# First part of both feed-forward stages: a buffer for each sum of squares, the roots taken together, the down weights split later, some sums and low parts on GpSimd

## The reference

```python
def rmsnorm(x, g, eps=1e-6):
    y = x * lax.rsqrt(jnp.mean(x * x, axis=-1, keepdims=True) + eps)
    return y * g

def swiglu(h, wg, wu, wd):
    return (jax.nn.silu(h @ wg) * (h @ wu)) @ wd
...
x = x + swiglu(rmsnorm(x, norm_ffn[layer]), w_gate[layer], w_up[layer], w_down[layer])
```

## Time and profile before

| | us |
|---|---|
| median of 3 runs (3134.54 to 3141.05) | 3136.88 |
| the profiled execution | 3135.46 |
| its span, first to last instruction | 3133.7 |

### The profile page before, as it was taken

One profiled execution on the slowest core, in us unless ns is written; L12 is line 12 of the kernel. 1 busy time (PEld: TensorE's weight loads), 2 busy tenths in 40 slices (PEclk: granted clock), 3 DMA queues, 4 the chain that ended last, 5 costly groups with the idle time before them and its releaser, 6 DMA issues. The chain is left out here.

```text
span 3133.7 us, 47003 instructions
## 1 busy us (share of the span) xinstructions
PE 2995.8 (96%) x18884; PEld 2917.1 (93%) x18884; DVE 1277.0 (41%) x2761; ACT 960.0 (31%) x1653; POOL 816.3 (26%) x434
## 2 busy tenths in 40 slices
PE   6999997999899999999989999999999999999998
PEld 5889987899899999999989999999889999999997
DVE  4423345566533333323353444444653333333334
ACT  4322234444521111111154444444452112111112
POOL 3211112111233222222232223322213223323220
PEclk8999998999999999999999999999999999999999
DMA  3122143110212111111021111111112111211101
GB/s 119 58 69 64 49 168 102 51 54 25 74 41 61 46 40 54 40 40 40 13 69 39 46 45 45 43 42 43 34 38 77 41 40 46 61 40 40 54 0 64
DMA packets 199615, 165.75 MB, mean 53 GB/s; under 512 B 9766, under 2 KB 182774, under 8 KB 199294
## 3 DMA queue, kind: packets, MB, share of 16 engines
q1 hardware_dynamic: 199486, 163.96, 17.3%
HBM read 140.78 MB, written 28.92 MB: 54 GB/s over the span
## 5 line engine op out<-in xcount | busy, mean ns | idle before, releaser
L1402 DVE TENSOR_TENSOR xT<-xT,ffn_banks 128x384 f32<-128x384 f32 (+1 forms) x528 | 280.0, 532 | 219.1 <-PE ffn_banks L238 218.6
L236 PE MATMUL ffn_banks<-hhi,ffn_whi 128*128 128x384 f32 (+1 forms) x1056 | 346.6, 328 | 12.4 <-DVE ffn_act L1382 12.4
L236 PE MATMUL ffn_banks<-hhi,whi 128*128 128x384 f32 (+1 forms) x1056 | 347.8, 329 | 4.1 <-DVEq L1367 3.7
L238 PE MATMUL ffn_banks<-hhi,wlo 128*128 128x384 f32 (+1 forms) x1056 | 346.2, 328 | 0.0
L236 PE MATMUL ffn_banks<-ffn_ahi,ffn_whi 128*128 128x384 f32 (+1 forms) x1056 | 344.7, 326 | 1.6 <-DVE xT L1402 1.6
L237 PE MATMUL ffn_banks<-hlo,whi 128*128 128x384 f32 (+1 forms) x1056 | 346.0, 328 | 0.0
L237 PE MATMUL ffn_banks<-hlo,ffn_whi 128*128 128x384 f32 (+1 forms) x1056 | 345.7, 327 | 0.0
L238 PE MATMUL ffn_banks<-hhi,ffn_wlo 128*128 128x384 f32 (+1 forms) x1056 | 345.5, 327 | 0.0
L238 PE MATMUL ffn_banks<-ffn_ahi,ffn_wlo 128*128 128x384 f32 (+1 forms) x1056 | 344.2, 326 | 0.0
L237 PE MATMUL ffn_banks<-ffn_alo,ffn_whi 128*128 128x384 f32 (+1 forms) x1056 | 344.1, 326 | 0.0
L1288 POOL TENSOR_TENSOR ffn_alo<-ffn_act,ffn_ahi 128x384 fp32r<-128x384 f32 (+1 forms) x132 | 127.9, 970 | 776.6 <-ACT ffn_ahi L1209 776.6
(11 more groups left out here) (363 smaller groups left out, 6740.1 us busy)
## 6 DMA issues: line engine op xcount, KB each, us to landing
ffn_up_st<-in_w_up SPq DMA_DIRECT2D x44, 512.0 KB, 3.8
ffn_down_st<-in_w_down SPq DMA_DIRECT2D x22, 1024.0 KB, 4.8
wst<-in_w_gate SPq DMA_DIRECT2D x24, 512.0 KB, 3.7
wst<-in_w_qkv SPq DMA_DIRECT2D x23, 512.0 KB, 4.4
wst<-in_w_in SPq DMA_DIRECT2D x22, 512.0 KB
ffn_gate_st<-in_w_gate SPq DMA_DIRECT2D x20, 512.0 KB
wst<-in_w_out SPq DMA_DIRECT2D x16, 512.0 KB
load_xin<-in_x_prompt SPq DMA_DIRECT2D x8, 512.0 KB, 4.8
```

Of the source, the lines that this page charges most:

```text
L236: nc.tensor.matmul(out, whi[:, k, :], hhi[:, k, c0:c0 + w], start=(k == 0), stop=False)
L238: last = nc.tensor.matmul(out, wlo[:, k, :], hhi[:, k, c0:c0 + w], start=False, stop=(k == kts - 1))
L1402: v.tensor_tensor(x, x, banks[:, 4 + k % 4, 0:w], ALU.add).then_inc(added, 1)
```

## The change

Part 0 of both feed-forward stages is put in another order on four engines.

- Each chunk's sum of squares has a buffer of its own: `acc`, and two that lie in the staging of the up weights (`up_st`). So the squares wait no longer for `total` of the chunk before. Instead ScalarE waits, ahead of the squares of chunk 1, for GpSimd's low parts of both up tiles, and SyncE sends the up weights of part 1 only when all three totals are made.
- ScalarE: squares of chunk 1, root 0, high parts of chunk 2, squares of chunk 2, roots 1 and 2 together; only then Silu and the high parts of the first chunk's hidden values. The split of the down weights stands between the two Silu of the second chunk.
- GpSimd: takes the low part of gate tile 1 (`split(0, 0, 1)`), which VectorE made, and the three sums of chunk 2. The low parts of the first chunk's hidden values stand ahead of the down weights' low part.
- TensorE: `total(1)` stands behind the first group of the second chunk and `total(2)` behind its second group.
- VectorE: the low parts of chunk 1 ahead of reciprocal 0, the sums of chunk 1 ahead of the first scaling, the low parts of chunk 2 and reciprocals 1 and 2 ahead of the first product.

```diff
@@ Rms.square
             if q == 0:
-                dst = self.acc
-                if i:
-                    act.wait_ge(self.summed, i)
+                dst, m = self.acc[i % len(self.acc)], len(self.acc)
+                if i >= m:
+                    act.wait_ge(self.summed, i - m + 1)
@@ Rms.add
-    def add(self, dve, i):
+    def add(self, engine, i, on):
...
-            a = self.acc[:, :, 0:w]
-            self.nc.vector.tensor_tensor(a, a, self.sq[n % 2][:, :, 0:w], ALU.add).then_inc(self.added, 1)
+            a = self.acc[i % len(self.acc)][:, :, 0:w]
+            on.tensor_tensor(a, a, self.sq[n % 2][:, :, 0:w], ALU.add).then_inc(self.added, 1)
@@ ffn_stage
-                  acc, [banks[:, 4], banks[:, 5]], r)
+                  [acc[:], *(up_st[:, f, 0:2 * W].rearrange("p (k n) -> p k n", n=W) for f in range(F))], [banks[:, 4], banks[:, 5]], r)
@@ SyncE, loads
                             sp.wait_ge(w_lo[m], lo_count(m, i - 1, f))
+                        if m and isinstance(i, int):
+                            sp.wait_ge(rms.summed, NC)
                         load(i, m, f)
@@ ScalarE
             for k in range(KT):
                 gained_high(nc, S, g0, k, order[1]).then_inc(x_hi, 1)
+            act.wait_ge(w_lo[1], lo_count(1, 0, F - 1))
+            rms.square(act, 1)
             rms.root(act, 0)
-            rms.square(act, 1)
             for k in range(KT):
                 gained_high(nc, S, g0, k, order[2]).then_inc(x_hi, 1)
+            rms.square(act, 2)
+            rms.root(act, 1)
+            rms.root(act, 2)
+            hidden(0, [0])
+            silu(0, 1, 0)
+            split_down(0)
+            silu(0, 1, 1)
             for f in range(F):
-                silu(0, 0, f)
-            for f in range(F):
-                high(0, 0, f)
-            rms.root(act, 1)
-            rms.square(act, 2)
-            split_down(0)
-            hidden(0, [1])
-            rms.root(act, 2)
+                high(0, 1, f)
             hidden(0, [2])
@@ GpSimd
+            split(0, 0, 1)
             for f in range(F):
                 split(0, 1, f)
+            rms.add(pool, 2, nc.gpsimd)
+            hidden(0, [0])
             split_down(0)
-            hidden(0)
+            hidden(0, [1, 2])
@@ TensorE
             for f in range(F):
                 for m in range(2):
                     group(0, 1, f, m)
-                rms.total(pe, 1 + f)
+                    if f == 0:
+                        rms.total(pe, 1 + m)
@@ VectorE
-            dve.wait_ge(w_hi[0], 1)
-            v.tensor_tensor(wlo[0][:, 1, :], gate_st[1], whi[0][:, 1, :], ALU.subtract).then_inc(w_lo[0], 1)
-            rms.add(dve, 0)
-            rms.reciprocal(dve, 0)
+            rms.add(dve, 0, v)
             for k in range(KT):
                 dve.wait_ge(x_hi, k + 1)
                 gained_low(nc, S, g0, k, order[1]).then_inc(x_lo, 1)
+            rms.reciprocal(dve, 0)
+            rms.add(dve, 1, v)
             dve.wait_ge(rms.rooted, 1)
             for f in range(F):
                 scale_gate(0, 0, f)
                 scale_up(0, 0, f)
-            rms.add(dve, 1)
-            for f in range(F):
-                multiply(0, 0, f)
             for k in range(KT):
                 dve.wait_ge(x_hi, KT + k + 1)
                 gained_low(nc, S, g0, k, order[2]).then_inc(x_lo, 1)
             rms.reciprocal(dve, 1)
-            rms.add(dve, 2)
-            dve.wait_ge(rms.rooted, 2)
+            rms.reciprocal(dve, 2)
+            for f in range(F):
+                multiply(0, 0, f)
+            dve.wait_ge(rms.rooted, 3)
+            dve.wait_ge(product, F)
             hidden(0, [1])
-            rms.reciprocal(dve, 2)
-            dve.wait_ge(rms.rooted, 3)
             hidden(0, [2])
```

More of the change, by code:

```diff
@@ L1043, in add @@
             n = 3 * i + q - 1
-            dve.wait_ge(self.squared, 4 * i + q + 1)
+            engine.wait_ge(self.squared, 4 * i + q + 1)
             if n:
-                dve.wait_ge(self.added, n)
-            a = self.acc[:, :, 0:w]
-            self.nc.vector.tensor_tensor(a, a, self.sq[n % 2][:, :, 0:w], ALU.add).then_inc(self.added, 1)
+                engine.wait_ge(self.added, n)
+            a = self.acc[i % len(self.acc)][:, :, 0:w]
+            on.tensor_tensor(a, a, self.sq[n % 2][:, :, 0:w], ALU.add).then_inc(self.added, 1)
     def total(self, pe, i):
@@ L1055, in total @@
         for k in range(2):
-            last = self.nc.tensor.matmul(self.means[i % n][:, 0:w], self.S["ones"][:], self.acc[:, k, 0:w],
+            last = self.nc.tensor.matmul(self.means[i % n][:, 0:w], self.S["ones"][:], self.acc[i % len(self.acc)][:, k, 0:w],
                                          start=(k == 0), stop=(k == 1))
@@ L1281, in split_down, with hidden @@
                 nc.gpsimd.tensor_tensor(flat[1], down_st[:], flat[0], ALU.subtract).then_inc(w_lo[2], 1)
-            def hidden(i):
-                for c, (c0, w) in enumerate(CH):
+            def hidden(i, cs=range(NC)):
+                for c in cs:
+                    c0, w = CH[c]
                     for f in range(F):
@@ L2428, in mix1_stage @@
         rms = Rms(nc, S, st, (0, 1, 2), [vflat[:, j * 2 * W:(j + 1) * 2 * W].rearrange("p (k n) -> p k n", n=W) for j in range(2)],
-                  otok[:].rearrange("p a n -> p (a n)")[:, 0:2 * W].rearrange("p (k n) -> p k n", n=W), [pP[:, 0], pP[:, 1]], r)
+                  [otok[:].rearrange("p a n -> p (a n)")[:, 0:2 * W].rearrange("p (k n) -> p k n", n=W)], [pP[:, 0], pP[:, 1]], r)
         block = st.block()
@@ L2853, in _ @@
             nc.vector.memset(nb[CHUNK:P, 0:CHUNK], BIG).then_inc(s["set_up"], 1)
-            rms.add(dve, 0)
+            rms.add(dve, 0, nc.vector)
             rms.reciprocal(dve, 0)
-            rms.add(dve, 1)
+            rms.add(dve, 1, nc.vector)
             for n, x in enumerate(ahead):
@@ L2859, in _ @@
                     rms.reciprocal(dve, 1)
-                    rms.add(dve, 2)
+                    rms.add(dve, 2, nc.vector)
                 if n == 4 * KT:
```

## The result

The changed kernel took 3118.3 us (median of 4 runs, 3117.07 to 3118.78) against 3138.1 us for the kernel before, run beside it: a ratio of 0.9939, 95% interval 0.9926 to 0.9952, that is 19 us less (by the ratio; by the medians 19.8). Its profiled span is 3117.0 us, 16.7 us shorter than before.

The account below looks back on a forecast made before the run. TensorE, busy for 96% of the span, was taken as the bound. Gains of 7.5 us in `ffn0` and 11.2 us in `ffn1`, together 18.7 us off 3136.9, gave 3118.2 us, range 3110 to 3126 us.

Parts of the forecast that it names:

- Both old waits go: TensorE's waits for `total(2)` and second-chunk `scale_up` vanish: 4.0 and 4.25 us in `ffn0`, 2.7 and 8.15 us in `ffn1`.
- on offer: TensorE's old waits plus half-clock losses in part 0, all that could be gained: 13.1 us in `ffn0`, 13.65 us in `ffn1`.
- The margin of 1.3 us: After `total(2)`, TensorE has 8.4 us of work to cover the 7.1 us until `scale_gate` of chunk 2 is done.
- GpSimd holds VectorE up: GpSimd's SBUF reads block VectorE at stage start: first sum near 1.8 us, first two low parts near 1.4 and 2.7 us.
- Side by side: Rival: GpSimd and VectorE don't hold each other up at stage start; gain 25.3 us, 3111.6 us; chance 0.20.
- The chain to `scale_gate`: From TENSOR_SCALAR to the first scaling, through root and table load, 6.8 us as in `mix1`, 0.5 shorter in `ffn0`.
- the new waits: TensorE waits for the first `scale_gate` in each stage: 4.25 us in `ffn0`, 2.45 us in `ffn1`.
- Clock: Half clock on TensorE behind the new waits: 1.7 us charged in `ffn0` (3.1 at most), nothing in `ffn1` (2.8 at most).
- GpSimd's sums: Third chunk's three adds on GpSimd, 1.85 us each for 768 columns; no wait at `total(2)` finally charged.
- The slower rival: GpSimd's three adds hold TensorE at `total(2)`; 5.5 us an add eats the gain, 6.6 us makes it 6 us slower; chance 0.04.
- Sum: Net gain in part 0: 7.5 us in `ffn0` and 11.2 us in `ffn1`, together 18.7 us, giving 3118.2 us.

Follow-up runs that it names:

- e8: e7 plus gate tile 1's low part back on VectorE and the third chunk's squares ahead of its high parts; 3116.4 us, 0.9938 of the kernel before.
- e5: The changed kernel with one more, unneeded GpSimd subtraction reading SBUF behind the up low parts; 3122.7 us in one run.
- e6: The changed kernel with an unneeded GpSimd fill with zeros, reading no SBUF tensor, behind the up low parts; 3119.2 us in one run.
- e9: e8 with VectorE's reciprocal 1 ahead of the third chunk's low parts and reciprocal 2 after four of them; 3116.0 us, 0.9914 of the kernel before.
- e7: The changed kernel with root 0 ahead of the second chunk's fourth square and the first scaling behind its first sum; 3118.5 us, 0.9940 of the kernel before.
- e10: The changed kernel measured again, unaltered, beside e9 on the same chip; 3125.3 us, 0.9947 of the kernel before.
- e3: The changed kernel with the third chunk's three sums on VectorE, behind that chunk's low parts; 3121.5 us, 0.9943 of the kernel before.
- e2: The changed kernel with one buffer for the three sums, as before the change; 3130.0 us, 0.9973 of the kernel before.

## Why the prediction was right

- **Both old waits go.** They went, with the half clock behind them: 13.1 and 13.65 us on offer. The margin of 1.3 us behind `total(2)` held in the changed kernel: `scale_gate` of chunk 2 ends 1.0 us before TensorE needs its bank in `ffn0` (838.50 against 839.49) and 1.3 us in `ffn1`. e8 shows how soon it is used up (3.4 us of waiting once the reciprocals came late).
- **GpSimd holds VectorE up.** Shown by the lengths (first sum 1.78 us, predicted 1.8; first two lows 4.15 us, predicted 1.4 + 2.7) and by e5 against e6. "Side by side" fell with it: 25 us were not reached, and e9, which takes the collisions and the chain out of TensorE's way, gets 13 us out of `ffn0` and 13.8 out of `ffn1`, all that was on offer.
- **The chain to `scale_gate`.** 6.7 us where the earlier trace rows gave 6.8; the new waits are 4.17 and 2.21 us, predicted 4.25 and 2.45. e7 shows that square, sum and table load are 2.8 us of it. Of the drain that the Trainium skill adds to a table load ("ScalarE: Activation LUTs", section "What ACT_TABLE_LOAD costs") the trace shows nothing again: load 2318.85 for 1.28, Sqrt at 2320.15.
- **Clock.** 1.7 us charged in `ffn0`, 1.7 us measured; nothing charged in `ffn1`, nothing measured. This was partly luck: in e10 the same kernel lost 1.6 us there as well, and 3.0 us in `ffn0`, close to the 3.1 that the prediction gave as the most.
- **GpSimd's sums.** 1.9 us an add of 768 columns, 1.6 of 640 (busy time by line), near the 1.85 that I took; with ScalarE's last square between them three take 6.0 us, and `total(2)` waited in neither stage. In `ffn0` it missed a wait by 0.3 us (the last sum ends at 829.54, `total(2)` starts at 829.87), and only because the half clock had made TensorE late, as the prediction has it. The slower rival needed 5.5 us an add.
- **Sum.** 7.5 and 11.2 us predicted, 7.9 and 11.4 measured; 3118.2 us predicted, 3118.3 measured. So close a hit has luck in it: medians of one kernel differ by 3 to 7 us from chip to chip here (before 3136.5 to 3143.0, changed 3118.3 and 3125.3). Two slips in the working change nothing: 827.6 against 826.7 is 0.9 us late, not 1.0; and the adds of `ffn1` start at 2331.2 in the slower rival, by which three of them end near 2335.8, not 2336.3.

## What to carry to other kernels

When an elementwise step moves to GpSimd, look at what VectorE does meanwhile: if both read their operands from SBUF, and VectorE's instruction has two of them there, VectorE's waited here until GpSimd's had ended, and the price was that wait, not GpSimd's slower pace. An instruction with one SBUF operand, such as the reciprocal of e9, can be put beside GpSimd's. When a wait on the busiest engine shrinks, look at the next thing in its list at once: here the first scaling, `total(2)` and the third chunk took the same 2 to 4 us over from one another until all three were early. Undo the parts one by one: one moved line alone gave about half of the gain, taking the separate buffers away lost about half, and the sums on GpSimd gave nothing that could be told.

## What the runs showed of the hardware

VectorE's instructions with two SBUF inputs that met a subtraction of GpSimd's ended 0.36 us (320 columns), 0.42 us (384) and 0.8 us (768) after it; a fill by GpSimd held up none, and a reciprocal beside its sums kept its length.

Every feed-forward stage starts with TensorE idle for 1.8 to 1.9 us. In 19 of the 24 starts of these twelve profiles the clock then fell to 1.2 GHz for a while and 1.6 to 1.7 us were lost; in 5 it did not. TensorE by stretches behind the start of `ffn1` and behind the next wait, in the changed kernel's first profile (wait 2.21 us):

```profile
2299.43:2307.50 8.07, 8.07 (x37) 0.79 0.47 130
2321.41:2328.00 6.59, 6.59 (x35) 1.00 0.01 2
```

and in its second, e10 (wait 3.81 us):

```profile
2304.00:2312.00 8.00, 8.00 (x47) 1.00 0.47 131
...
2325.93:2332.00 6.07, 6.07 (x25) 0.72 0.01 3
```

In these two profiles the loss moved: where the start kept 2.4 GHz, TensorE reached the next wait 1.6 us earlier, stood longer, and the clock fell behind that one instead. It is no rule: in `ffn0` of the changed kernel the clock fell behind both, and a wait of 2.2 us in `ffn1` was followed by 1.2 GHz in e3 and not in the changed kernel, e2 and e6. So the length of a wait alone does not tell how quick the part is, and one profile's part 0 says nothing below 2 to 3 us. What decides whether the clock falls behind a gap of about 2 us stays open.
